# A weight item of the next stage multiplied in pieces inside a norm's tail

## The reference

```python
for l in range(2):
    h = rms_norm(x, norm1[l])
    proj = h @ w_in[l]                    # queries, keys, values, gates of four kinds of heads
    x = x + mixed(proj) @ w_out[l]
    h2 = rms_norm(x, norm2[l])
    x = x + jnp.square(jax.nn.relu(h2 @ w_up[l])) @ w_down[l]
x = rms_norm(x, final_norm)
...
mod = jax.nn.silu(c) @ ada_w + ada_b
shift, scale, gate = jnp.split(mod, 3, axis=-1)
h = rms_norm_2(x, norm_w) * (1.0 + scale[:, None]) + shift[:, None]
proj = h @ w_in_2
```

## Time and profile before

| | |
|---|---|
| median of 3 runs | 2240.09 us (2239.44 to 2240.71) |
| the profiled execution's own time | 2239.29 us |
| its span, first to last instruction | 2237.4 us |
| PE busy | 2074.2 us (93%) |
| DVE / ACT / POOL busy | 1118.8 / 847.5 / 198.4 us |
| mean granted clock of PE | 0.954 |

### The profile page before, as it was taken

The page is one execution under the profiler, slowest core; times in us unless marked ns, Lnnn a source line. Parts: engine busy times, 40 slices in busy tenths (PEclk is TensorE's granted clock), DMA queues, the critical chain, the costliest instruction groups (busy, mean ns, idle before and its releaser), DMA issues. The chain is left out here.

```text
span 2237.4 us, 27050 instructions
## 1 busy us (share of the span) xinstructions
PE 2074.2 (93%) x10240; PEld 1679.5 (75%) x10244; DVE 1118.8 (50%) x1967; ACT 847.5 (38%) x1760; POOL 198.4 (9%) x169
## 2 busy tenths in 40 slices
PE   6898999999999889899899999799898998999988
PEld 5686677887888778677788787678787897777666
DVE  4677534432433478653462353568765332325544
ACT  4344643321332334563331232354432335325522
POOL 1331000000000143000100000002031330000100
PEclk8998999999999999799999999999999999999999
DMA  5321012332332332002452344132224223331231
GB/s 176 90 81 48 2 47 66 94 104 85 94 113 76 109 102 70 20 1 66 151 186 96 115 140 132 36 126 85 76 72 133 72 75 104 113 94 29 76 132 57
DMA packets 177522, 198.25 MB, mean 89 GB/s; under 512 B 38755, under 2 KB 140786, under 8 KB 176882
## 3 DMA queue, kind: packets, MB, share of 16 engines
q1 hardware_dynamic: 177394, 196.53, 28.8%
HBM read 180.74 MB, written 11.55 MB: 86 GB/s over the span
## 5 line engine op out<-in xcount | busy, mean ns | idle before, releaser
L151 DVE TENSOR_TENSOR weight_pairs<-weight_ring,weight_pairs 128x1024 fp32r<-128x1024 f32 (+4 forms) x293 | 357.4, 1222 | 504.0 <-ACT weight_pairs L142 503.3
L172 PE MATMUL psum<-operand,weight_pairs 128*128 128x512 f32 x1320 | 535.0, 405 | 45.0 <-PEq L194 32.4
L142 ACT ACTIVATE weight_pairs<-weight_ring 128x1024 fp32r<-128x1024 f32 (+4 forms) x293 | 302.7, 1036 | 612.5 <-PE psum L174 576.6
L174 PE MATMUL psum<-operand,weight_pairs 128*128 128x512 f32 x1320 | 532.6, 403 | 0.0
L173 PE MATMUL psum<-operand,weight_pairs 128*128 128x512 f32 x1320 | 531.9, 403 | 0.0
L172 PEld LDWEIGHTS psum<-operand,weight_pairs 128*128 128x128 f32 x1320 | 258.0, 195 | 113.5 <-issue 43.6
L173 PEld LDWEIGHTS psum<-operand,weight_pairs 128*128 128x128 f32 x1320 | 253.6, 192 | 56.6 <-issue 1.8
L174 PEld LDWEIGHTS psum<-operand,weight_pairs 128*128 128x128 f32 x1320 | 252.8, 192 | 56.0 <-issue 0.8
L173 PE MATMUL psum<-weight_pairs,hidden 128*128 128x512 f32 x512 | 202.1, 395 | 0.0
L172 PE MATMUL psum<-weight_pairs,hidden 128*128 128x512 f32 x512 | 200.5, 392 | 0.0
L174 PE MATMUL psum<-weight_pairs,hidden 128*128 128x512 f32 x512 | 199.1, 389 | 0.0
(11 more groups left out here) (412 smaller groups left out, 2727.0 us busy)
## 6 DMA issues: line engine op xcount, KB each, us to landing
weight_ring<-in_w_in_dram SPq DMA_DIRECT2D x100, 512.0 KB, 3.7
weight_ring<-in_w_up_dram SPq DMA_DIRECT2D x64, 512.0 KB, 3.7
weight_ring<-in_w_down_dram SPq DMA_DIRECT2D x64, 512.0 KB, 3.6
weight_ring<-in_w_out_dram SPq DMA_DIRECT2D x24, 512.0 KB, 3.6
ada_rows<-in_ada_w_dram SPq DMA_DIRECT2D x24, 512.0 KB, 4.6
spilled<-v_t SPq DMA_DIRECT2D x22, 256.0 KB, 4.3
weight_ring<-in_w_in_dram SPq DMA_DIRECT2D x20, 256.0 KB, 2.9
weight_ring<-in_w_proj_a_dram SPq DMA_DIRECT2D x8, 512.0 KB, 3.4
```

The source lines that it names most:

```text
L142: act.activation(self.pairs[:, i % SPLIT_RING, 0, 0:n], self.buf[:, i % RING, 0:n], ACT.Copy).then_inc(self.rounded, 1)
L151: dve.tensor_tensor(self.pairs[:, i % SPLIT_RING, 1, 0:n], self.buf[:, i % RING, 0:n], self.pairs[:, i % SPLIT_RING, 0, 0:n].bitcast(F32), ...
L172: pe.matmul(out, lhs[0], rhs[0], start=start, stop=False)
L174: return pe.matmul(out, lhs[1], rhs[0], start=False, stop=stop)
```

## The change

The first item of the next stage is multiplied in three pieces by tokens. LATER is tokens 0 to 255, LATEST 256 to 383, LAST 384 to 511. PE's queue at the end of a tail becomes: turn of tile 2, LATER, turn of tile 3, LATEST. LAST opens the next stage, which then takes the item as used. The pieces go to banks 4 and 5 (bank 6 for the gates' 16 rows). For that, `half_mlp` counts its banks from 4 and swaps the banks of its two down products, and `front` of layer 1 uses banks 4 and 5 for its first pair of tiles. ACT's and DVE's queues in the tail are not touched.

```diff
     def take(self, pe):
+        pair = self.next(pe)
+        self.taken += 1
+        return pair
+
+    def next(self, pe):
         i = self.taken
-        self.taken += 1
         pe.wait_ge(self.split, i + 1)
...
+LATER, LATEST, LAST = slice(0, 2 * P), slice(2 * P, 3 * P), slice(3 * P, S)
...
             if t and self.operand is not None:
                 self.turn(pe, t - 1)
         if self.operand is not None:
-            self.turn(pe, T - 1)
+            for rows in (LATER, LATEST):
+                if rows == LATEST:
+                    self.turn(pe, T - 1)
+                pe.wait_ge(self.high_rows, 2 * rows.stop // P)
+                pe.wait_ge(self.low_rows, 2 * rows.stop // P)
+                begin(pe, rows)
...
+def item_by_channels(pe, psum, banks, w, pair, k, chunks, rows):
+
+    for h, bank in enumerate(banks):
+        for kk in range(w[0].shape[1]):
+            mm = product(pe, psum[:, bank, rows], [w[j][:, kk, h * P:(h + 1) * P] for j in (0, 1)],
+                         [pair[:, k + kk, j, rows] for j in (0, 1)], start=(k + kk == 0 and rows.start == 0),
+                         stop=(k + kk == chunks - 1))
+    return mm
+
+BEGUN = (4, 5)
+
+def begin_channels(psum, weights, pair):
+    def begin(pe, rows):
+        item_by_channels(pe, psum, BEGUN, weights.next(pe), pair, 0, KD, rows)
+    return begin
...
+        mm = item_by_channels(pe, psum, banks, w, pair, k, chunks, LAST if begun and i == 0 else slice(0, S))
...
-                product_by_tokens(pe, psum, 4 * c, weights, hidden, per_half, n, low)
+                product_by_tokens(pe, psum, 4 * (1 - c), weights, hidden, per_half, n, low)
...
+        def bank(slot, h):
+            return BEGUN[h] if begun and slot == 0 else 2 * (slot % 2) + h
...
                     elif kind == "tokens":
+                        if i == 0 and which == "A" and begun:
+                            pe.wait_ge(raw_stored, 2)
...
+def gate_product(pe, psum, w, pair, rows):
+
+    for k in range(KD):
+        mm = product(pe, psum[0:2 * H, GATE_ROWS, rows], [w[j][:, k, :] for j in (0, 1)], [pair[:, k, j, rows] for j in (0, 1)],
+                     start=(k == 0 and rows.start == 0), stop=(k == KD - 1 and rows == LAST))
+    return mm
...
-            w = weights.take(pe)
-            for k in range(KD):
-                mm = product(pe, psum[0:2 * H, ROWS, :], [w[j][:, k, :] for j in (0, 1)],
-                             [turned_x[:, k, j, :] for j in (0, 1)], start=(k == 0), stop=(k == KD - 1))
-            weights.used(mm)
+            weights.used(gate_product(pe, psum, weights.take(pe), turned_x, LAST))
```

More of the change, by code:

```diff
@@ L478, in low, with products @@
             rest.then_inc(self.low_rows, 1)
+LATER, LATEST, LAST = slice(0, 2 * P), slice(2 * P, 3 * P), slice(3 * P, S)
 class Residual(Norm):
-    def products(self, pe, start, lhs, chunks, per_half, written=None, freed=None, between=None):
+    def products(self, pe, start, lhs, chunks, per_half, written=None, freed=None, between=None, begin=None):
         psum, weights = self.psum, self.weights
@@ L831, in product_by_tokens, with product_by_channels @@
     return k
-def product_by_channels(pe, psum, banks, weights, pair, chunks):
+def item_by_channels(pe, psum, banks, w, pair, k, chunks, rows):
[10 more added lines that the diff above has]
+    return begin
+def product_by_channels(pe, psum, banks, weights, pair, chunks, begun=False):
     k = 0
@@ L881, in _ @@
         def _(pe):
-            tail.products(pe, start, lhs, chunks, per_half)
+            tail.products(pe, start, lhs, chunks, per_half, begin=begin_channels(psum, weights, lhs))
         @block.scalar
@@ L966, in layers @@
                                    sb("position_table", [P, TABLE_W], ctx)[:], table_rows,
-                                   sb("latent_t", [P, 3, 2, S], ctx, F32R)[:], sb("gate_work", [P, 3, S], ctx)[:], best, select)
+                                   sb("latent_t", [P, 3, 2, S], ctx, F32R)[:], sb("gate_work", [P, 3, S], ctx)[:], best, select, l > 0)
             mixed = operand
@@ L990, in layers @@
                            (a["final_norm"].rearrange("(o d) -> o d", o=1) if last else a["norm1"][l + 1:l + 2, :]),
+                           (begin_gates if last else begin_channels)(psum, weights, operand),
                            besides[1])
@@ L1041, with __init__ @@
     B = 3
-    def __init__(self, psum, weights, turned_x, hidden, n, work, start, sems):
+    def __init__(self, psum, weights, turned_x, hidden, n, work, start, sems, begun=False):
+        self.begun, self.bank = begun, (lambda f: (f + BEGUN[0]) % 8 if begun else f % 8)
         self.psum, self.weights, self.turned_x, self.hidden, self.n, self.start = psum, weights, turned_x, hidden, n, start
@@ L1052, in products @@
                 pe.wait_ge(self.rectified, f - 6)
-            product_by_channels(pe, self.psum, (f % 8, f % 8 + 1), self.weights, self.turned_x, KD)
+            product_by_channels(pe, self.psum, (self.bank(f), self.bank(f + 1)), self.weights, self.turned_x, KD,
+                                self.begun and f == 0)
     def round_square(self, act, f):
@@ L1067, in rectify @@
                     act.wait_ge(self.squared, g - B + 1)
-                act.activation(self.relu[:, g % B, :], self.psum[:, g % 8, :], ACT.Relu).then_inc(self.rectified, 1)
+                act.activation(self.relu[:, g % B, :], self.psum[:, self.bank(g), :], ACT.Relu).then_inc(self.rectified, 1)
                 if g >= 1:
@@ L1103, in half_mlp @@
             rectified, squared, high, low, summed, masked), nc.Block() as block:
-        up = UpProjection(psum, weights, turned_x, hidden, n, work, start, (rectified, squared, high, low))
+        up = UpProjection(psum, weights, turned_x, hidden, n, work, start, (rectified, squared, high, low), begun=True)
         @block.sync
@@ L1140, in _, with final_half_mlp @@
                     cols = slice(c * 512, (c + 1) * 512)
-                    dve.tensor_tensor(x[:, t, cols], psum[:, 4 * c + t, :], x[:, t, cols], ALU.add).then_inc(summed, 1)
-def final_half_mlp(nc, psum, x, weights, operand, hidden, n, work, per_half, ident, eps, small, gain_row, beside=None):
+                    dve.tensor_tensor(x[:, t, cols], psum[:, 4 * (1 - c) + t, :], x[:, t, cols], ALU.add).then_inc(summed, 1)
+def final_half_mlp(nc, psum, x, weights, operand, hidden, n, work, per_half, ident, eps, small, gain_row, begin, beside=None):
     start = weights.taken
@@ L1214, in _ @@
             up.products(pe)
-            tail.products(pe, down, hidden, n, per_half, low, ((rectified, n - 4), (rectified, n)), rows_between)
+            tail.products(pe, down, hidden, n, per_half, low, ((rectified, n - 4), (rectified, n)), rows_between, begin)
         @block.scalar
@@ L1289, in front @@
 def front(nc, psum, weights, operand, turned, values, lat, gates, chosen, gains, forget_bias, gate_forms, small, ident, causal,
-          table, table_rows, latent_t, gate_work, best, select):
+          table, table_rows, latent_t, gate_work, best, select, begun):
     base = weights.taken
@@ L1385, in dense @@
                             free(slot)
[L1386 to L1390, removed]
+                        rows = LAST if begun and slot == 0 and i == 0 else slice(0, S)
+                        mm = item_by_channels(pe, psum, (bank(slot, 0), bank(slot, 1)), w, operand, i * (KD // 2), KD, rows)
                     elif kind == "tokens":
+                        if i == 0 and which == "A" and begun:
+                            pe.wait_ge(raw_stored, 2)
                         if i == 0 and which == "B":
@@ L1502, in dense @@
                         for h, tile in enumerate(PAIR_TILES[which]):
-                            act.activation(turned[:, tile, :], psum[:, 2 * (slot % 2) + h, :], ACT.Copy).then_inc(raw_stored, 1)
+                            act.activation(turned[:, tile, :], psum[:, bank(slot, h), :], ACT.Copy).then_inc(raw_stored, 1)
                     elif kind == "tokens" and last:
@@ L1805, in second_masks, with begin_gates, begin @@
     return build
+GATE_ROWS = 6
+def gate_product(pe, psum, w, pair, rows):
[3 more added lines that the diff above has]
+    return mm
+def begin_gates(psum, weights, pair):
+    def begin(pe, rows):
+        gate_product(pe, psum, weights.next(pe), pair, rows)
+    return begin
 def convolved_heads(nc, psum, weights, turned_x, q_t, k_t, v_t, k_tok, v_tok, decay, beta_t, tok_cols, last_decay, conv_cols,
@@ L1823, in convolved_heads @@
     N = 3 * H
-    NB, ROWS, TB = 4, 6, (4, 5, 7)
+    NB, ROWS, TB = 4, GATE_ROWS, (4, 5, 7)
     LAG, REDUCE, NSQ = 4, 5, 4
```

## The result

The changed kernel takes 2257.65 us (median of 4 runs, 2256.56 to 2259.25) against 2239.77 us for the kernel before: a ratio of 1.0074, with a 95% interval from 1.0062 to 1.0086. In a later set of runs it was 1.0072 (1.0057 to 1.0088). It is slower by 17.9 us, not by the 6.9 us forecast, and lies above the stated range.

A forecast was written before the change was run, and what follows sets the result against it. PE, busy 93% of the span, was taken to be bound by its idle time and half-clock time. Tail terms 1.86 + 2.06 + 3.16 - 0.21 gave +6.9 us, so 2247.0 us, range 2238 to 2255.

The forecast's parts named there:

- LATER waits for DVE's split, not for the rows: In the tails, LATER cannot use the first pause; it starts about 0.05 us after DVE's split of the weight item.
- A0: Tail behind the attention output of layer 0; forecast +1.86 us.
- B0: Tail behind the second half of layer 0's feed-forward part; forecast +3.16 us.
- A1: Tail behind the attention output of layer 1; forecast +2.06 us.
- The turn and all behind it are pushed back, PE is last at the boundary: In three tails tile 3's turn waits behind LATER, and PE, not DVE, ends the tail; 10.03 or 10.40 us at full clock.
- 128-wide products at 0.111: Price of each LATEST and LAST matmul, 0.111 us, making 2.66 us for each piece of 24.
- B1: Tail behind the second half of layer 1's feed-forward part, with a 16-column item; forecast -0.21 us.
- The low clock costs the mean of what it costs now, 2.04 us: Clock term in each tail: one fall in the pause before LATER, costing 2.04 us, bounds 0 and 2.64.
- The rest of the diff costs nothing: Outside the tails' pieces, swapped banks and layer 1's added wait were claimed to add no time.
- The rival in which the clock comes out anew everywhere: Later pauses shift and clock falls come out anew throughout, making it faster: 2234.8 us or less; chance 0.10.
- the dearer case: Narrow matmuls at 0.222 us add 16 us, 2263 us; or the clock falls badly elsewhere, about 2258; chance 0.10.
- the rival with cheap ones at 0.06: 128-wide matmuls in the tails take 0.06 us each; total +2.1 us, 2242.2 us, no change; chance 0.14.

The follow-up runs named there:

- wide_again: Changed kernel with LATEST replaced by tokens 0 to 255 multiplied again into unread spare banks, LAST being tokens 256 to 511; 2248.17 us, 1.0036 to the kernel before.
- the fastest kernel: Changed kernel with the first weight item's conversion moved earlier and two pieces of 256 tokens in place of three; 2222.29 us, 0.9915 to the kernel before.

## Why the prediction was right in direction and wrong in size

- **LATER waits for DVE's split, not for the rows: right.** It starts 0.14 us behind the split's end (361.81 to 361.95), in A0, B0 and A1 6.16 us behind the start of tile 2's turn. Moving only the conversion brings it to 2.17 us and turns +0.72% into -0.32%, which shows this cause by itself.
- **The turn and all behind it are pushed back, PE is last at the boundary: right.** The sum from the split's end to item 2 was 12.07 us in A0. It is 374.69 - 361.81 = 12.88, and the 0.8 us more are LAST's.
- **128-wide products at 0.111: right.** LATEST's 24 starts lie (370.17 - 367.57) / 23 = 0.113 us apart. The Trainium skill ("TensorE: Matmul & The Clock Gate", Back-to-back issue gap) has 81 ns there; this trace disagrees, and the measurement decides. Only with the gates' 16 weight columns are they cheaper:

```profile
1477.61 0.22 PE L176 MATMUL psum<-operand,weight_pairs 128*16 128x128 f32 x1
...
1477.79 0.23 PE L176 MATMUL psum<-operand,weight_pairs 128*16 128x128 f32 x1
...
1477.97 0.22 PE L176 MATMUL psum<-operand,weight_pairs 128*16 128x128 f32 x1
...
1481.77 0.22 PE L176 MATMUL psum<-operand,weight_pairs 128*16 128x128 f32 x1 [2.74 <-PEq L198]
...
1484.18 0.80 PE L176 MATMUL psum<-operand,weight_pairs 128*128 128x512 f32 x1
```

  From each of the first three rows to the next there are three matmuls, so 0.06 us a matmul with 16 weight columns against 0.113 with 128. Halving the columns that stream, from 256 to 128, changes the spacing only from 0.118 to 0.113. So for this type it is the columns of the weights, not those that stream, that set the pace there. The last two rows are the start and the end of B1's LAST, 2.41 us, held by the second item's split as forecast.
- **"The low clock costs the mean of what it costs now, 2.04 us": this step failed.** For the fall in the pause it was about right: LATER took 366.78 - 361.95 = 4.83 us in A0 where 2.83 is full speed, a cost of 2.0, and over the four tails that fall cost 2.0, 2.8 (with the turn, which in B0 still ran in it), 1.9 and 1.4 us, mean 2.0. What the step left out is that the clock falls a second time, in the middle of dense work. It took "one pause followed by dense work as before" for granted, and LATEST and LAST are not like the 512-wide work of before: 128-wide products kept PE busy without keeping the clock up. Up to item 2 the second fall made LAST 0.82, 0.36 and 0.95 us longer in A0, B0 and A1, and the sum came to 9.0 us where 6.9 were forecast. Another 6.9 us (2.44, 1.33, 2.32 and 0.85) fell on the second and third items, which the sum did not look at. Together the second falls cost 9.1 us, and the tails' 15.9 us are 9.0 above the forecast. wide_again shows the cause: same order, same pauses in three of the tails, wider moving operand, no second fall. What it is about narrow products that brings the clock down was not tried: the wider pieces also stream more columns in the same time, and no run separates the two.
- **The rest of the diff costs nothing: right** (0.9994).
- **B1 even: right, in part by luck.** -0.21 us was forecast up to item 2. It was -0.88 there, since the first fall cost 1.4 us and not 2.04, and the second fall brought it to -0.03 up to item 3.
- The rival in which the clock comes out anew everywhere had the sign wrong, and the dearer case gave this time (2258) with no mechanism behind it: it put the cost "elsewhere", and nearly all of it lies directly behind the tails. That its number fits is luck. Its other case, narrow matmuls at 0.222, and the rival with cheap ones at 0.06 are refuted by the 0.113.
- **Smaller slips in the working.** A pause longer than LATER's 5.1 us was there already: in B1 of the kernel before PE idles 5.76 us ahead of the turn of tile 3. The turn costs 0.79 us (366.78 to 367.57), not 0.87, and the row named for it gives (1.09 - 0.27) / 7 = 0.117 a transpose, not 0.109. A clock cost of 1.5 to 2.64 us a tail and 3 us either way give 2241.8 to 2252.4 us, not 2244.6 to 2253. Of the signs named, the turn of tile 3 came 7.25 us later against its scaling, as the sum implies, and not some 5; the first item was done in 3.48 us behind the boundary and not in 2.7.

## What to carry to other kernels

Before work is put into a pause, look up on every queue when its last input is ready: here the rows were there 6 us before the weights, and the piece filled the wrong pause and delayed the turn. Once its input was moved as well, the same idea gained 0.32%, and with two pieces in place of three 0.85%. Here it paid to cut the product so that no piece is narrow: three pieces of 256, 128 and 128 columns took 8.3 us of PE at full clock (2.83 and twice 24 x 0.113) for 5.6 us of work and cost the clock behind them as well, two pieces of 256 took 2.93 us each in the fastest kernel (357.53 to 360.46, 363.81 to 366.74). And when a sum contains the clock, follow it beyond the edited stretch until the granted clock is the same in both.

## What the runs showed of the hardware

The granted clock can fall while PE never pauses for longer than 0.8 us: in the changed kernel at 373.1 us, behind some 40 matmuls of 128 columns, with PE busy 5.93 of the 6.70 us ahead. With 256 columns in their place it stayed at 2.4 GHz. Both a pause (5.1 us ahead of LATER) and narrow dense work came before a fall here. A pause of 2.31 or 2.69 us between 256-wide products and the turn on one side and 256-wide products on the other left the clock up in A0 and B0 of the fastest kernel; in A1, behind a pause of 2.34 us in the same order, it fell for 3.4 us. A matmul of float32r with 128 weight columns starts 0.113 us behind the last one at 128 moving columns and 0.118 us at 256; with 16 weight columns it is 0.06 us at 128.
